# Seven products instead of eight in the down projections of three MLPs

## The reference

```python
def sq_relu_mlp(u, w1, w2):
    return jnp.square(jax.nn.relu(u @ w1)) @ w2
...
h = post_norm_residual(h, sq_relu_mlp(modulate(h, sh2, sc2), mlp_w1[i], mlp_w2[i]), g2, ln_g[i, 1], ln_b[i, 1])
...
h = h + jnp.square(jax.nn.relu(u @ w_up[l])) @ w_down[l]
```

## Time and profile before

| | us |
|---|---|
| median of 3 runs | 3605.13 (3602.18 to 3605.29) |
| the profiled execution, its device time | 3603.14 |
| its span, first to last instruction | 3601.3 |
| granted TensorE clock, mean | 0.958 |

### The profile page before, as it was taken

How to read it: one execution, slowest core, us unless ns; L and a number is a source line. 1 busy time by engine, 2 the same in 40 slices (tenths; PEclk the granted TensorE clock), 3 DMA queues, 4 the chain that set the end, 5 groups by cost and what they waited for, 6 DMA issues and landing times.

```text
span 3601.3 us, 37151 instructions
## 1 busy us (share of the span) xinstructions
PE 3307.9 (92%) x15223; PEld 2729.6 (76%) x15223; DVE 1868.8 (52%) x2623; ACT 1142.3 (32%) x1679; POOL 443.7 (12%) x261
## 2 busy tenths in 40 slices
PE   7999887979999999778799999997986899999997
PEld 3888776758888888667688888886875688888886
DVE  4624677665555544676544434355775633333334
ACT  4311786252121122342411111125345432222222
POOL 0101563210000000313000000011570000000000
PEclk9999999989999999889899999998987999999998
DMA  6434220203333331010111111111120111111111
...
DMA packets 190996, 237.97 MB, mean 66 GB/s; under 512 B 9672, under 2 KB 149563, under 8 KB 190827
## 3 DMA queue, kind: packets, MB, share of 16 engines
...
...
## 4 chain that ended last, share of the span: by engine, by line
PE 75%; DVE 13%; ACT 7%; issue 3%; DMA 1%; POOL 0%; SPq 0%; DVEq 0%; ACTq 0%; POOLq 0%
PE psum L520 24%; PE psum L521 24%; PE psum L522 24%; DVE small L636 2%; ACT temp L807 2%; DVE small L1266 1%; DVE H L1371 1%; ACT U_hi L526 1%; DVE PT_lo L531 1%; DMA raw<-in_ada_w_dram 1%; ACT prob L1232 1%; DVE small L661 1%; DVE split L531 1%; ACT split L526 1%; PE psum L797 1%
## 5 line engine op out<-in xcount | busy, mean ns | idle before, releaser
L520 PE MATMUL psum<-U_hi,split 128*128 128x512 f32 x2108 | 836.1, 397 | 61.9 <-DVE split L531 37.6
L521 PE MATMUL psum<-U_lo,split 128*128 128x512 f32 x2108 | 830.3, 394 | 0.0
L522 PE MATMUL psum<-U_hi,split 128*128 128x512 f32 x2108 | 829.1, 393 | 0.0
L526 ACT CAST split<-raw 128x1024 fp32r<-128x1024 f32 x260 | 266.5, 1044 | 1275.3 <-PE psum L522 875.6
L520 PE MATMUL psum<-split,A_hi 128*128 128x512 f32 x1536 | 600.0, 391 | 3.0 <-ACT temp L807 3.0
L522 PE MATMUL psum<-split,A_lo 128*128 128x512 f32 x1536 | 599.1, 390 | 0.0
L521 PE MATMUL psum<-split,A_hi 128*128 128x512 f32 x1536 | 599.0, 390 | 0.0
L1371 DVE TENSOR_TENSOR H<-H,psum 128x512 f32<-128x512 f32 x416 | 281.3, 686 | 588.6 <-PE psum L522 588.6
L520 PEld LDWEIGHTS psum<-U_hi,split 128*128 128x128 f32 x2108 | 401.9, 191 | 154.3 <-DVE split L531 38.9
L531 DVE TENSOR_TENSOR split<-raw,split 128x1024 fp32r<-128x1024 f32 x260 | 324.6, 1263 | 283.8 <-ACT split L526 283.5
L522 PEld LDWEIGHTS psum<-U_hi,split 128*128 128x128 f32 x2108 | 401.7, 191 | 85.0
...
## 6 DMA issues: line engine op xcount, KB each, us to landing
raw<-in_mlp_w_dram SPq DMA_DIRECT2D x128, 512.0 KB, 4.5
raw<-in_ada_w_dram SPq DMA_DIRECT2D x96, 512.0 KB, 4.4
raw<-in_w_in_dram SPq DMA_DIRECT2D x38, 512.0 KB, 4.0
raw<-in_w_up_dram SPq DMA_DIRECT2D x32, 512.0 KB, 4.2
raw<-in_w_down_dram SPq DMA_DIRECT2D x32, 512.0 KB, 4.3
H<-in_x_dram ACTq DMA_DIRECT2D x8, 512.0 KB, 6.8
...
```

Of the source, the lines that this page charges most:

```text
L520: pe.matmul(out, l_hi, r_hi, start=start, stop=False)
L521: pe.matmul(out, l_hi, r_lo, start=False, stop=False)
L522: return pe.matmul(out, l_lo, r_hi, start=False, stop=stop)
L526: return act.copy(hi, src).then_inc(*k.hi.inc(*key))
```

## The change

- In blocks 0 to 6 of each MLP the down product (1024 tokens x 512 inner x 1024 outputs) is cut in quarters and made of 7 products by Strassen's algorithm in Winograd's form, in the order 1, 2, 6, 7, 5, 4, 3 (`pe_products`). A product has 4 token tiles x 2 inner chunks x 3 passes = 24 matmuls. Products 1, 6, 5, 3 go on in the same four banks, and DVE reads them in between. Block 7 keeps the form before.
- Sums of activation quarters are made by DVE (`dve_fold`, 8 operations of 128x512 a block), sums of weight quarters by POOL (`pool_products`, 4 operations of 128x1024). POOL also gates the down units and takes the low parts of the weight sums 7, 5, 4 and 3; ACT casts all high parts; DVE takes the low parts of weights 1, 2, 6 and of all activations, and 28 additions of 128x512 into `H` (16 before).
- The square is made by ACT. The up tiles of block 0 come in another order, with the gate row ahead of the third.
- Units of an MLP land in the page that later holds their low part, and SP waits until that page is free (`place_mlp_unit`). The same holds for the first three units of the Fourier stage and of in2. Of the units split ahead for the next stage, the first is split behind down tile 0, and the raw pages of the third and fourth are freed by the down units of block 7.
- The 48 `ada_w` units of layer 1 are loaded by ACT's queue into spare pages and summed at fixed places of MLP0's blocks 1 to 6 (`ADA_LOAD_AT`, `ADA_SUM_AT`; 8 stands for the place behind product 7).
- in2 leaves out the meta tokens for its last four units (the gelu gate), whose scratch in DRAM shrinks from 1040 to 1024 columns.

The core of the diff:

```diff
-                for j in range(FB):
-                    up(w1, (blk * FB + j) * P)
-                    ada_units(beside if blk else 0)
-                for j in range(FB):
-                    down(w2, (blk * FB + j) * P, gate)
-                    ada_units(beside if blk else 0)
+                roles = [("u", 0), ("u", 1), ("d", 0), ("d", 1), ("d", 2), ("d", 3), ("u", 2), ("u", 3)]
+                for what, j in sorted(roles, key=lambda r: r[0] == "d") if blk == 0 else roles:
+                    if what == "u":
+                        up(w1, (blk * FB + j) * P)
+                    else:
+                        down(w2, (blk * FB + j) * P, gate)
+                    units[-1].spot = (name, blk, what, j)
...
+        slots = dict(zip(range(mix, mix + 8), (0, 1, 2, 3, 4, 0, 1, 2)))
+        slots.update(zip(range(fout - 4, fout + 8), (3, 4, 0, 1, 2, 3, 4, 0, 1, 2, 4, 0)))
+        slots.update(zip(range(in2, in2 + 24), (3, 4, 0, 1, 2, 3, 4, 0, 1, 2, 3, 4, 0, 1, 3, 2, 4, 0, 1, 3, 2, 4, 0, 1)))
+        in_place = [fout - 4 + i for i in range(3)] + [in2 + i for i in range(3)]
...
+    def place_mlp_unit(self, u, left):
+
+
+        name, blk, what, j = u.spot
+        if what == "u":
+            hi, lo = self.slot_pages((3, 4, 1, 2)[j] if blk == 0 else 3 + j % 2)
+        else:
+            hi, lo = 2 * FB - 3 + j, j
+        u.page = lo
+        u.raw = self.page[:, lo].rearrange("p a n -> p (a n)")
+        u.left_by = left[lo]
+        if what == "d" and blk < BLOCKS - 1:
+            left[lo] = [("product", (name, blk), "5" if j < 2 else "3")]
+            left[hi] = [("product", (name, blk), "3")]
+            if j == 0:
+                left[FB] = [("product", (name, blk), "6")]
+            return
+        self.parts_at(u, hi, lo)
+        u.before = left[hi]
+        left[hi] = left[lo] = [("done", u.s)]
...
 
     if blk == 0:
-        return [(i, c) for c in range(NCH) for i in range(FB)]
+        return [(0, 0), (1, 0), (2, 0), (3, 0), (2, 1), (3, 1), (0, 1), (1, 1)]
...
+PRODUCTS = ("1", "2", "6", "7", "5", "4", "3")
+CHAIN = ("1", "6", "5", "3")
+QUARTER = {"1": (0, 0), "2": (0, 0), "6": (1, 0), "7": (1, 1), "5": (1, 1), "4": (1, 0), "3": (0, 1)}
+QUARTER_BEGINS = {"1": None, "2": "1", "6": None, "7": None, "5": "7", "4": "6", "3": None}
...
+def pe_products(k, pe, on, stage):
+    at = k.banks.n
+    for p in PRODUCTS:
+        on.wait_ge(*k.lo.at("act", stage, p))
+        on.wait_ge(*(k.lo if p in ("1", "2", "6") else k.pool_lo).at("weight", stage, p))
+        a_hi, a_lo, w_hi, w_lo = act_part(k, p, 0), act_part(k, p, 1), weight_part(k, p, 0), weight_part(k, p, 1)
+        for t in range(TPC):
+            s = slice(t * P, (t + 1) * P)
+            b = k.banks.take(on, ("product", stage, p, t), (k.h_added, (stage, p, t)),
+                             slot=(at + t + (0 if p in CHAIN else TPC)) % 8)
+            for j in range(2):
+                m = three_passes(pe, k.psum[:, b, :], a_hi[:, j, s], a_lo[:, j, s], w_hi[:, j, :], w_lo[:, j, :],
+                                 p in ("1", "2", "7") and j == 0, j == 1, read_between=True)
+            m.then_inc(*k.down_done.inc(stage, p, t))
+    k.banks.n = (at + TPC) % 8
+
...
+def act_high_parts(k, act, on, stage, p, weights):
+
+    if weights:
+        on.wait_ge(*k.pool_folded.at(stage, {"3": "4"}.get(p, p)))
+    elif p == "4":
+        on.wait_ge(*k.squared.at(stage, FB - 1, 1))
+    else:
+        on.wait_ge(*k.folded.at(stage, p, 1))
+    on.wait_ge(*k.product_done(stage, PAGE_OF[p]))
+    hi, src = (weight_part(k, p, 0), weight_sum(k, p)) if weights else (act_part(k, p, 0), act_sum(k, p))
+    act_hi(k, act, on, hi, src, "weight" if weights else "act", stage, p)
...
+BEHIND_TILE = {1: ("1", "u2"), 3: ("2", "u3"), 5: ("next",)}
+BEHIND_TILE_FIRST = {4: ("1",), 5: ("2",), 6: ("next",)}
+BEHIND_TILE_LAST = {1: ("d0", "u2"), 2: ("d1",), 3: ("u3",), 4: ("d2",), 5: ("next", "d3")}
...
+ADA_LANDS = ("land", "sum", 6, 7, "land", "sum", "land", "land")
+ADA_LOAD_AT = {0: (0, 1, 2, 3), 2: (4, 5), 5: (6,), 8: (7,)}
+ADA_SUM_AT = {1: (0, 1), 2: (2, 3), 4: (4, 5), 7: (6,), 8: (7,)}
...
+            square = k.act_page[:, FB + i if last else i, c]
+            on.wait_ge(*k.relu_done.at(stage, i, c))
+            act.activation(square, k.temp[t][:], ACT.Square).then_inc(*k.squared.inc(stage, i, c))
             on.wait_ge(*k.squared.at(stage, i, c))
...
-        if name == "mlp0" and blk == BLOCKS - 1:
...
+                act_hi(k, act, on, k.A_hi[:, i, c * CH:(c + 1) * CH], k.act_page[:, FB + i, c], "a", stage, i, c)
...
+                act_hi(k, act, on, act_part(k, "12"[i // 2], 0)[:, i % 2, :], k.act_page[:, i, 0], "a", stage, i)
+            act_behind_tile(k, act, on, stage, q)
+        if not last:
+            act_weights(k, act, on, unit_after(k, name, blk, 1))
+            for p in ("6", "7", "5", "4", "3"):
+                act_high_parts(k, act, on, stage, p, True)
+                act_high_parts(k, act, on, stage, p, False)
+                if p == "7":
+                    act_ada_parts(k, act, on, stage, 2 * FB)
+            continue
+        ahead = [s for s in (unit_after(k, name, blk, j) for j in (1, 2, 3, 4)) if s]
+        if name == "mlp0":
             act_gate_row(k, act, on, 1, 0)
         for tt in range(TT):
+            if tt == 1:
...
+def dve_fold(k, dve, on, stage, j):
+
+    a, total = k.act_page, k.sum_page[:, j]
+    on.wait_ge(*k.ada_x_ok.now())
+    on.wait_ge(*k.lo.at("a", stage, j))
+    on.wait_ge(*k.lo.at("a", stage, j + 2))
+    dve.tensor_tensor(total, a[:, j, 1], a[:, j + 2, 1], ALU.add).then_inc(*k.folded.inc(stage, "5", j))
+    on.wait_ge(*k.folded.now())
+    dve.tensor_tensor(a[:, j, 1], a[:, j, 0], a[:, j, 1], ALU.subtract).then_inc(*k.folded.inc(stage, "7", j))
+    on.wait_ge(*k.folded.now())
+    dve.tensor_tensor(a[:, j, 0], total, a[:, j, 0], ALU.subtract).then_inc(*k.folded.inc(stage, "6", j))
+    on.wait_ge(*k.folded.now())
+    dve.tensor_tensor(a[:, j + 2, 0], a[:, j + 2, 0], a[:, j, 0], ALU.subtract).then_inc(*k.folded.inc(stage, "3", j))
+
...
+LOW_AT = {("2", 0): "6", ("2", 3): "7", ("6", 0): "5", ("6", 2): "4", ("7", 0): "3"}
...
+                s = slice(c * CH, (c + 1) * CH)
+                dve_lo(k, dve, on, k.A_lo[:, i, s], square, k.A_hi[:, i, s], "a", stage, i, c)
+            elif c == 0:
+                p = "12"[i // 2]
+                dve_lo(k, dve, on, act_part(k, p, 1)[:, i % 2, :], square, act_part(k, p, 0)[:, i % 2, :], "a", stage, i)
+                if i % 2:
+                    k.lo.also("act", stage, p)
+            elif (i < 2) == (blk == 0):
+                dve_fold(k, dve, on, stage, i % 2)
+            dve_behind_tile(k, dve, on, stage, q)
+            if name == "mlp0" and blk >= 2 and q == 0:
+                dve_mod(k, dve, on, 1, blk - 2)
+        if not last:
+            if blk:
+                ready = lambda tt: on.wait_ge(*k.h_added.at((name, blk - 1), "3", TPC - 1))
+            else:
+                ready = lambda tt: on.wait_ge(*before.hat(k, tt))
+            for p in PRODUCTS:
+                for t in range(TPC):
+                    dve_quarter_tile(k, dve, on, stage, p, t, 1.0 if blk else alpha, ready)
+                    if (p, t) == ("2", 0):
+                        on.wait_ge(*k.pool_folded.at(stage, "4"))
+                        dve_lo(k, dve, on, weight_part(k, "6", 1), weight_sum(k, "6"), weight_part(k, "6", 0), "weight",
...
+def pool_products(k, pool, on, name, gate):
...
+        b11, b12, b21, b22, n = (k.page[:, 0:2, 0], k.page[:, 0:2, 1], k.page[:, 2:4, 0], k.page[:, 2:4, 1], k.page[:, FB])
+        for j in range(FB):
+            u = mlp_unit(k, name, blk, "d", j)
+            on.wait_ge(*k.landed(u))
+            if gate:
+                on.wait_ge(*k.gate_ok.at(*gate))
+                pool.tensor_tensor(u.raw, u.raw, k.row_gate[:], ALU.mult).then_inc(*k.pool_gated.inc(u.s))
+        if gate:
+            on.wait_ge(*k.pool_gated.now())
+        if blk:
+            on.wait_ge(*k.product_done((name, blk - 1), "6"))
+        on.wait_ge(*k.lo.at("weight", stage, "1"))
+        pool.tensor_tensor(b11, b12, b11, ALU.subtract).then_inc(*k.pool_folded.inc(stage, "5"))
+        on.wait_ge(*k.pool_folded.now())
+        pool.tensor_tensor(n, b22, b11, ALU.subtract).then_inc(*k.pool_folded.inc(stage, "6"))
+        on.wait_ge(*k.pool_folded.now())
+        pool.tensor_tensor(b12, b22, b12, ALU.subtract).then_inc(*k.pool_folded.inc(stage, "7"))
+        on.wait_ge(*k.lo.at("weight", stage, "2"))
+        on.wait_ge(*k.pool_folded.now())
+        pool.tensor_tensor(b21, b21, n, ALU.subtract).then_inc(*k.pool_folded.inc(stage, "4"))
+        on.wait_ge(*k.pool_folded.now())
+        for p in ("7", "5", "4", "3"):
+            on.wait_ge(*k.hi.at("weight", stage, p))
+            pool.tensor_tensor(weight_part(k, p, 1), weight_sum(k, p), weight_part(k, p, 0).bitcast(F32),
```

(57 more changed lines are left out.)

375 lines of the change are left out of this document (259 added, 116 removed).

## The result

| | before | changed |
|---|---|---|
| median (us) | 3605.21 | 3586.09 |
| lowest to highest | 3602.18 to 3605.91 | 3582.48 to 3588.47 |
| span of the profiled execution | 3601.3 | 3582.5 |
| busy PE, DVE, ACT, POOL | | 3223.6, 2196.4, 1387.6, 1063.4 |

The ratio is 0.995, with a 95% interval of 0.9935 to 0.9965: 19 us faster, where 45.6 had been forecast. The time lies inside the range of 3488 to 3602 and outside this case's own of 3545 to 3573.

What follows compares the result with a forecast made beforehand. The PE bounds it: a block lasts as long as its matmuls stream. -114.3 for matmuls, +33.8 and +44.4 for product 6, +2.4, -11.9 give -45.6: 3559.5 us; own range 3545 to 3573, whole range 3488 to 3602.

Steps and rivals of the forecast that it cites:

- The matmuls removed: Down products of 7 blocks in 3 MLPs: 504 matmuls fewer, 5.44 us for a tile of 24, 114.3 us saved.
- Sums of element work cost nothing: In the blocks, added DVE, ACT and POOL work stays below the PE's 81.6 us, so sums alone cost nothing.
- The place: Ahead of product 6: POOL's turn on memory delays DVE's activations 6; PE waits 2.25 us in 15 blocks, +33.8 us.
- E: The moment at which the PE has issued the last up tile; product 6 is wanted at E + 10.9.
- MLP0: Product 6 in blocks 1 to 6: POOL comes first twice; wait 5.2 us plus 2.2 of lower clock, +44.4 us.
- The clock behind 2.25 us: After product 6's 2.25 us waits: no fall to the lower clock assumed, 1.7 us each as upper bound.
- Behind MLP0: Transition after MLP0: the PE's 7.51 us wait for a split unit shrinks by earlier splitting, -4 us (bounds 2 and 8).
- From MLP1 to MLP2: Transition: -4.4 us from a DMA landing sooner behind MLP1, -3.5 us from in2 losing four meta products.
- Rival 3: The clock falls behind the 2.25 us stalls at product 6 too: 25 us more, 3585 us; chance 0.12.
- Rivals 1 and 2: Rival 1: in MLP0 DVE gets its turn first, wait 2.7 us instead of 5.2 with its clock; 3531 us, chance 0.17.
- rival 2: POOL and DVE don't meet ahead of product 6: 0.3 us in 15 blocks, 1.5 in 6; 3492 us, chance 0.18.
- Rival 4: Chain to product 6 grows by one more POOL turn in every block, waits 5 to 6 us; 3634 us, chance 0.10.

Runs made afterwards that it cites:

- both edits: Changed kernel with POOL's low part of weights 7 waiting for activations 6 and the seventh `ada_w` sum moved behind product 6: 3488.07 us.
- The run with the split late: First Fourier unit split behind all down tiles of MLP0 as before the change, against the 3488 us version with both edits: 3490.43 us.
- 3495 us with one wait: Changed kernel with one wait added: POOL takes the low part of weights 7 only after DVE's low part of activations 6: 3494.97 us.

## Why the prediction was right or wrong

- **The matmuls removed: right.** 5.44 us a block, seen bare as 43.68 - 38.24. (The 0.2265 us a matmul is MLP1's row, 2759 in 625.0 us; 385 in 87.0 give 0.226.)
- **Sums of element work cost nothing: right, for the reason given.** No engine is near the PE's time; what the products lost was order and the clock behind it: with the order mended (both edits) they take 38.3 to 38.4 us, and 38.9 in each MLP's first block.
- **The place: right.** Among the products only product 6 waits, and no up tile of blocks 1 to 6 by more than 0.4 us. 1.96 us in 12 blocks and 2.4 in three, for the forecast's 2.25: 30.8 us in place of 33.8. To start again costs some 0.3 us more than the row of the wait shows: a block with a wait of 1.96 us and no fall takes 40.50 us, 2.26 more than 38.24, so each block lost what was forecast. The activations were ready at E + 13.0 (2063.66, with 2050.7 for E), forecast E + 13.1.
- **MLP0: right at product 6.** 4.73 us of wait for 5.2, and with the clock 7.2 us a block for 7.4 (45.4 us on average - 38.24). The loss at up unit 2 is 0.7 us a block (45.73 us of up tiles for 45.06), 0.4 forecast. What was missed is the gate row in the last block, counted at 0: with it the stretch behind block 6 is 4.0 us shorter (PE's wait of 4.85 us fell to 3.28, and less of the lower clock follows it). So the stretch's 8.3 us for 11.0 hold misses both ways: 4.0 us better here, 1.6 us worse by a fall of the clock in block 0.
- **The clock behind 2.25 us: wrong, and the step that failed.** "I take no fall" rested on one row against another, and the row chosen was the less like this place. It isn't one stall of 2.31 us but a wait of 2.21 us and a remainder, among matmuls of 16 columns, 1.7 us behind the end of another stretch at 0.50 (PE before the change):

```profile
2736.97 0.28 PE L520 MATMUL psum<-U_meta_hi,split 128*128 128x16 f32 x1 [2.21 <-DVE U_meta_lo L531]
```

The row with the fall, 1613.46, stands like product 6 behind matmuls of 256 and 512 columns without a break. 10 of 12 waits of 1.96 us and 2 of 3 of 2.4 us were followed by one: 12 x 1.6 = 19 us. The 8.5 and 10.1 us by which MLP1 and MLP2 missed are 11 of these falls, 17.6 us, and 1 us more. With 1.7 for each of 15 the range had it; as the likeliest case it should have been weighed over the two rows, not decided by one.
- **Behind MLP0: right in sum, by luck.** -3.2 for -4.0, but not by the step named. The wait of 7.51 us fell to 1.2, and around it 9.76 grew to 11.73 and 5.41 to 10.05: the four last 31.5 us for 30.9. The run with the split late gives the split 0.5 us. About half of the 3.2 us lies in the down tiles of MLP0's last block (44.6 us for 46.3, without a wait in either), where the mean clock is 0.98 for 0.94, behind a wait of 3.28 us in place of 4.85; where the other half comes from is open.
- **From MLP1 to MLP2: wrong, 10.6 us of the miss.** Both named gains are there, nearly whole. The wait of 15.59 us is 12.22 (-3.4, forecast -4.4), and the end of in2 comes 3.4 us sooner (187.5 for 190.9 us from there, forecast -3.5). They were added up as if the rest stood still. Given back were 2.3 us at the boundary, whose norm the moved split delays (put back, the stretch is 3.4 us shorter), 3.3 us in the 73 matmuls behind, at a lower clock whose cause stays open, and 3.8 us from there to MLP2, where a load that came sooner met another (kept apart, 2.7 us less).
- **The rivals.** Rival 3 said 3585 and 3586 was measured, but part of that is chance: its clock term of 25 us was 19, and the rest is the miss between MLP1 and MLP2. Rivals 1 and 2 didn't occur; rival 2 exists as a version (3495 us with one wait, 3492 forecast for it by a sum that leaves out the 2.4 us of MLP0's up units). Rival 4 was built and is 3625 us (3634 forecast); whether 0.3 us more of chain would do, as I wrote, no run tells, 1.3 us does. There are no table loads in the MLPs.

The Trainium skill, "SBUF — State Buffer", section "Who interferes with whom", gave the rule that the order of asking decides. The runs agree with it in both directions: 0.05 us ahead, VectorE has the turn and takes 1.22 us, 0.76 us behind (2059.50 and 2060.26) it takes 3.40.
